# A hybrid pool and RWKV-7 block in float32: output and second feed-forward products by seven block products, tokens on partitions

## The reference

```python
mixed = (g_pool * y_pool + g_rwkv * y_rwkv) @ w_out[l]
x = layer_norm(ALPHA * x + (1 + gt1) * mixed, ln1_g[l], ln1_b[l], LN_EPS)
h = x * (1 + sc2) + sh2
f = jnp.square(jax.nn.relu(h @ w_ff1[l])) @ w_ff2[l]
x = layer_norm(ALPHA * x + (1 + gt2) * f, ln2_g[l], ln2_b[l], LN_EPS)
```

## Time and profile before

| | us |
|---|---|
| median of 3 runs (lowest, highest) | 1109.46 (1108.66, 1114.62) |
| the profiled execution's own time | 1106.47 |
| its span, first to last instruction | 1104.7 |
| PE busy | 999.9 (91%) |
| DVE busy | 517.9 (47%) |
| ACT busy | 413.8 (37%) |
| POOL busy | 401.8 (36%) |
| mean granted clock of PE | 0.957 |

### The profile page before, as it was taken

The page is one execution under the profiler, slowest core; times in us unless marked ns, Lnnn a source line. Parts: engine busy times, 40 slices in busy tenths (PEclk is TensorE's granted clock), DMA queues, the critical chain, the costliest instruction groups (busy, mean ns, idle before and its releaser), DMA issues.

```text
span 1104.7 us, 25425 instructions
## 1 busy us (share of the span) xinstructions
PE 999.9 (91%) x10997; PEld 798.8 (72%) x10997; DVE 517.9 (47%) x620; ACT 413.8 (37%) x500; POOL 401.8 (36%) x236
## 2 busy tenths in 40 slices
PE   1898998898899889997999999889999999999992
PEld 1676777685677678675688888768888888888881
DVE  6636589377748768743231245746112112112217
ACT  0335354356335532524433224375124224214311
POOL 6333412311311131125253443445434434443422
PEclk9799999999999899998899999879999999999996
DMA  9322333223323324321433543304333333333201
GB/s 370 106 77 63 97 117 102 79 79 94 93 79 98 103 60 118 105 76 39 133 100 101 160 114 107 95 1 132 97 94 97 96 96 91 99 95 93 79 1 76
DMA packets 153641, 108.08 MB, mean 98 GB/s; under 512 B 5395, under 2 KB 145601, under 8 KB 153537
## 3 DMA queue, kind: packets, MB, share of 16 engines
q1 hardware_dynamic: 143729, 83.46, 25.9%
q10 hardware_dynamic: 9808, 23.08, 6.9%
HBM read 100.23 MB, written 2.10 MB: 93 GB/s over the span
## 4 chain that ended last, share of the span: by engine, by line
PE 47%; DVE 4%; DMA 1%; ACT 1%; issue 0%; SPq 0%; POOL 0%; DVEq 0%; ACTq 0%; POOLq 0%
PE set L1757 23%; PE bank L1757 20%; PE bank L1859 1%; PE set L1859 1%; DVE G L1319 1%; DMA w_raw<-in_w_rwkv_up_dram 1%; DVE xt L1388 1%; DVE xt L1390 1%; PE set L1821 0%; DVE t L1304 0%; PE set L1838 0%; PE set L1607 0%; PE set L1606 0%; DVE aa L1322 0%; DVE stat L1348 0%
## 5 line engine op out<-in xcount | busy, mean ns | idle before, releaser
L560 POOL TENSOR_TENSOR w_lo<-w_raw,w_hi 128x1024 fp32r<-128x1024 f32 (+2 forms) x87 | 200.4, 2303 | 439.2 <-ACT w_hi L641 399.2
L616 POOL TENSOR_TENSOR w_lo<-w_raw,w_hi 128x1024 fp32r<-128x1024 f32 x48 | 115.8, 2413 | 145.9 <-ACT w_hi L936 145.7
L1460 PE MATMUL bank<-h_hi,w_hi 128*128 128x512 f32 x256 | 109.3, 427 | 2.1 <-POOL w_lo L560 2.0
L641 ACT ACTIVATE w_hi<-w_raw 128x1024 fp32r<-128x1024 f32 (+2 forms) x75 | 75.5, 1006 | 82.9 <-PE set L1757 43.6
L669 ACT ACTIVATE Q<-set 128x1024 f32<-128x1024 f32 x56 | 57.4, 1026 | 130.7 <-PE set L1514 73.8
L936 ACT ACTIVATE w_hi<-w_raw 128x1024 fp32r<-128x1024 f32 x60 | 63.7, 1061 | 110.7 <-PE bank L1757 53.9
L1460 PE MATMUL bank<-h_hi,w_lo 128*128 128x512 f32 x256 | 103.3, 403 | 0.3 <-issue 0.3
L1460 PE MATMUL bank<-h_lo,w_hi 128*128 128x512 f32 x256 | 103.5, 404 | 0.0
L1355 DVE TENSOR_TENSOR f<-t 128x512 f32<-128x512 f32 x32 | 26.4, 825 | 125.9 <-ACT t L945 125.5
L1757 PE MATMUL bank<-h_hi,w_hi 128*128 128x512 f32 x192 | 76.5, 398 | 0.0
L1757 PE MATMUL set<-y_hi,w_hi 128*128 128x512 f32 x192 | 76.1, 396 | 0.0
(11 more groups left out here) (328 smaller groups left out, 2030.3 us busy)
## 6 DMA issues: line engine op xcount, KB each, us to landing
w_raw<-in_w_ff_dram SPq DMA_DIRECT2D x64, 512.0 KB, 3.9
w_raw<-in_w_in_dram SPq DMA_DIRECT2D x46, 512.0 KB, 3.8
y<-in_w_ada_dram ACTq DMA_DIRECT2D x20, 512.0 KB, 4.0
ada<-in_w_ada_dram SPq DMA_DIRECT2D x16, 512.0 KB, 9.6
Q<-in_w_ada_dram ACTq DMA_DIRECT2D x12, 512.0 KB, 4.3
w_raw<-in_w_rwkv_up_dram SPq DMA_DIRECT2D x8, 512.0 KB, 4.3
w_raw<-in_w_out_dram SPq DMA_DIRECT2D x8, 512.0 KB, 3.8
xtok<-in_x_dram SPq DMA_DIRECT2D x4, 512.0 KB, 9.9
```

Of the source, the lines that this page charges most:

```text
L560: link(pool.tensor_tensor(part_of(k, w_lo), part_of(k, w_raw), part_of(k, w_hi).bitcast(F32), ALU.subtract), "lo_ready")
L616: again(pool.tensor_tensor(part_of(k, w_lo), part_of(k, w_raw), part_of(k, w_hi).bitcast(F32), ALU.subtract), "lo_ready")
L641: link(act.activation(part_of(k, w_hi), part_of(k, w_raw), ACT.Copy), "hi_ready")
L1460: mm = pe.matmul(o, w, hx, start=(m == 0), stop=(m == 3 * KT - 1))
```

## The change

**Products.** A 2 x 2 block product is made with seven block products in place of eight. w_out and w_ff2 are cut in units of 512 rows (two units for w_out, eight for w_ff2). A unit's weight is four blocks B11, B12, B21, B22 of 256 x 512 (`load_quarter`, 128 x 1024 in SBUF), and the activations of the unit four blocks by halves of tokens and of rows. Seven sums of each (`FORMS` of weights, seven forms in `a_hi`, `a_lo`) are multiplied. Now the activations are held (128 x 128) and 512 weight columns move, so that tokens are on partitions in the result: 2 token rows x 2 k-tiles x 3 = 12 matmuls for one of the seven, 84 in a unit. A result stays in PSUM and is added to `res` by DVE after each product, to two places in all (`take`, two for each product), so banks are kept open over several products and PE waits for the take between (`FREED_BY`). `FORMS` are split in high and low as the chunks were.

**The order of a feed-forward unit.** PE: four chunks of w_ff1 (24 matmuls each), then the seven products in the order of `PRODUCTS`. There are three slots for `w_hi`/`w_lo`. For each hidden chunk ACT makes ReLU and square and the high parts (`highs`), DVE the sums of token halves and the low parts (`lows`). DVE also multiplies the four weight blocks by the gate row 1 + gt2, which was done on the result before (`scaled`), and makes T1 to T4 (`summed`). Each of these eight is a 128 x 1024 operation on two tiles of SBUF. The first unit stands outside of the loop and also adds the residual, with DVE and POOL.

**Order at the output product.** Its unit 0 comes after n = 5 of the up projections and unit 1 after n = 7. x is loaded straight into `res` and scaled by ACT. Layer norm 1 is made on token rows (`statistics`, `spreads`, `columns`), x hat is turned by PE (32 transposes) and h2 made from that; layer norm 2 likewise, without turning back.

**The tail of the scan.** In the last round the group statistics are made in slot 0, right behind `o_taken`. PE also makes the two gate rows there (`spread_gate`, 8 small matmuls each), and ACT copies them. SP issues the first three weight chunks ahead of the `wmix` tiles; the two broadcast rows are issued later.

```diff
+        FORMS = ("B11", "B21", "T2", "T1", "T3", "B22", "T4")
+        NFORM = len(FORMS)
+        QUARTERS = dict(B11=(3, 0, 0), B12=(4, 0, 1), B21=(5, 1, 0), B22=(6, 1, 1))
+        FORM_RAW = dict(B11=3, B21=5, T2=3, T1=8, T3=4, B22=6, T4=5)
...
+        FIRST_SLOT, SLOT = (1, 2, 0, 2, 0, 1, 2, 0, 1, 2, 0), (1, 2, 1, 2, 0, 1, 2, 0, 1, 2, 0)
+        BEFORE = (8 - PER, 9 - PER, 0, 1, 10 - PER, 2, 3, 4, 5, 6, 7)
+        CHUNK_RAW = (0, 1, 2, 7)
...
+        PRODUCTS = ((0, 4), (2, 0), (5, 4), (4, 6), (1, 4), (6, 6), (3, 4))
+        OPENS = (True, True, False, True, False, False, False)
+        FREED_BY = (6, None, 0, 5, 2, 3, 4)
+        READ_INTO = ((0, 0), (0, 0), (0, 1), (2, 1), (2, 1), (0, 1), (2, 0))
+        SUMS = ("B11", "B12", "B22", "B21", "T1", "T3", "T2", "T4")
+        NSUM = len(SUMS)
+        A_READY = ((1, 3), (2, 4), (5, 7), (5, 7), (6, 8), (6, 8), (6, 8))
...
+            for k in range(K_UP, K_UP + 3):
+                load_chunk(sp, k)
             for g in range(GP):
                 sp.dma_start(wmix[:, g, :], pool_mix[0, g]).then_inc(sem("wmix_in"), 16)
-            sp.dma_start(acc2[:, :], ln2_g.to_broadcast([P, D])).then_inc(sem("ln2_in"), 16)
-            sp.dma_start(ada2[:, :], ln2_b.to_broadcast([P, D])).then_inc(sem("ln2_in"), 16)
-            for k in range(K_UP, K_FF + 2 * KT):
+            for name in ("B11", "B12", "B22", "B21"):
+                load_quarter(sp, 0, name, w_out, 0)
...
+            with pool.Fori(0, NU - 1) as q:
+                again = loop_link(pool, counts, q, {"lo_ready": PER}, "pool_step")
+                for m in range(PER):
+                    pool.wait_ge(sem("hi_ready"), q * PER + (K_FF + PER + m + 1))
+                    raw = w_raw[CHUNK_RAW[m] if m < 4 else FORM_RAW[FORMS[m - 4]]]
+                    again(pool.tensor_tensor(w_lo[SLOT[m]][:, :, :], raw[:, :, :], w_hi[SLOT[m]][:, :, :].bitcast(F32), ALU.subtract), "lo_ready")
...
+            def highs(link, n, base, units=0, per=0):
+
+                i = n % 2
+                if n % 4 < 2:
+                    link(act.activation(a_hi[:, 0, i, :], left[:, i, 0:S // 2], ACT.Copy), "a_hi")
+                    act.wait_ge(sem("a_summed"), units * 4 + (n + 1))
+                    link(act.activation(a_hi[:, 1, i, :], a_sum[:, 0, :], ACT.Copy), "a_hi")
+                else:
+                    link(act.activation(a_hi[:, 2:4, i, :], halves(right[:, :]), ACT.Copy), "a_hi")
+                    act.wait_ge(sem("a_summed"), units * 4 + (n + 1))
+                    link(act.activation(a_hi[:, 4:7, i, :], a_sum[:, 1:4, :], ACT.Copy), "a_hi")
...
+            with act.Fori(0, NU - 1) as q:
+                again = loop_link(act, counts, q, {"hi_ready": PER, "relu": 4, "hidden_raw": 4, "a_hi": 8}, "act_step")
+                for m in range(2):
+                    split_again(again, m, q, 1)
+                for m in range(4):
+                    relu_of(again, m, q, 1)
+                    for k in {0: (2,), 1: (3, 4), 2: (5,), 3: (6,)}[m]:
+                        split_again(again, k, q, 1)
+                    highs(again, 12 + m, 0, q)
+                for m in range(7, PER):
+                    split_again(again, m, q, 1)
...
+                if it == QUADS and s == 0:
+                    link(dve.tensor_reduce(gn[:, 0, :], blocks16(O), AX_X, ALU.add))
+                    link(dve.tensor_scalar(gn[:, 0, :], gn[:, 0, :], 1.0 / N, None, ALU.mult))
+                    link(dve.tensor_tensor(blocks16(O), blocks16(O), gn[:, 0, :].unsqueeze(2).to_broadcast([P, 16, N]), ALU.subtract), "centred")
+                    dve.wait_ge(sem("o_squared"), it)
+                    link(dve.tensor_reduce(gn[:, 1, :], blocks(At), AX_X, ALU.add))
+                    link(dve.tensor_scalar(gn[:, 1, :], gn[:, 1, :], 1.0 / N, GN_EPS, ALU.mult, ALU.add), "o_var")
+                    dve.wait_ge(sem("o_std"), it)
+                    link(dve.reciprocal(gn[:, 3, :], gn[:, 2, :]))
+                    link(dve.tensor_tensor(blocks16(O), blocks16(O), gn[:, 3, :].unsqueeze(2).to_broadcast([P, 16, N]), ALU.mult), "o_normed")
...
+            def lows(link, n, units=0):
+
+                i = n % 2
+                x0, x1 = left[:, i, 0:S // 2], left[:, i, S // 2:S]
+                if n % 4 < 2:
+                    link(dve.tensor_tensor(a_sum[:, 0, :], x0, x1, ALU.subtract), "a_summed")
+                    dve.wait_ge(sem("a_hi"), units * 8 + (2 * n + 1))
+                    link(dve.tensor_tensor(a_lo[:, 0, i, :], x0, a_hi[:, 0, i, :].bitcast(F32), ALU.subtract), "a_low")
+                    dve.wait_ge(sem("a_hi"), units * 8 + (2 * n + 2))
+                    link(dve.tensor_tensor(a_lo[:, 1, i, :], a_sum[:, 0, :], a_hi[:, 1, i, :].bitcast(F32), ALU.subtract), "a_low")
+                else:
+                    link(dve.tensor_tensor(a_sum[:, 1, :], x1, right[:, S // 2:S], ALU.add))
+                    link(dve.tensor_tensor(a_sum[:, 2, :], a_sum[:, 1, :], x0, ALU.subtract))
+                    link(dve.tensor_tensor(a_sum[:, 3, :], right[:, 0:S // 2], a_sum[:, 2, :], ALU.subtract), "a_summed")
+                    dve.wait_ge(sem("a_hi"), units * 8 + (2 * n + 1))
+                    link(dve.tensor_tensor(a_lo[:, 2:4, i, :], halves(right[:, :]), a_hi[:, 2:4, i, :].bitcast(F32), ALU.subtract), "a_low")
+                    dve.wait_ge(sem("a_hi"), units * 8 + (2 * n + 2))
+                    link(dve.tensor_tensor(a_lo[:, 4:7, i, :], a_sum[:, 1:4, :], a_hi[:, 4:7, i, :].bitcast(F32), ALU.subtract), "a_low")
...
+            def scaled(link, name, unit, units=0):
+
+                raw, _, z = QUARTERS[name]
+                dve.wait_ge(sem(f"w_in{raw}"), units * 16 + 16 * (unit + 1))
+                row = (gate1 if unit < 2 else gate2)[:, z * S:(z + 1) * S].unsqueeze(1).to_broadcast([P, 2, S])
+                link(dve.tensor_tensor(two_by(w_raw[raw]), two_by(w_raw[raw]), row, ALU.mult), "summed")
...
+                if name == "T1":
+                    if unit == 3:
+                        dve.wait_ge(sem("lo_ready"), units * PER + (K_UNIT[2] + FORMS.index("T1") + 1))
+                    elif unit:
+                        lo_of("T1", unit - 1)
+                    link(dve.tensor_tensor(made("T1"), b12, made("B11"), ALU.subtract), "summed")
+                elif name == "T3":
+                    link(dve.tensor_tensor(made("T3"), made("B22"), b12, ALU.subtract), "summed")
+                elif name == "T2":
+                    lo_of("B11", unit)
+                    link(dve.tensor_tensor(made("T2"), made("B22"), made("T1"), ALU.subtract), "summed")
+                else:
+                    lo_of("B21", unit)
+                    link(dve.tensor_tensor(made("T4"), made("B21"), made("T2"), ALU.subtract), "summed")
...
+                link(dve.tensor_tensor(res[:, j, half], bank[PRODUCTS[at][1] + row], res[:, j, half], ALU.add), "taken")
...
+            def last_takes(link, unit, stage, units=0):
+
+                for at in range(NFORM - 1):
+                    for row in range(2):
+                        take(link, unit, at, row, units)
+                    if at in (1, 4, 5):
+                        j, z = READ_INTO[at]
+                        statistics(j, z)
+                        statistics(j + 1, z)
+                spreads(0)
+                columns(0, stage)
+                for row in range(2):
+                    take(link, unit, NFORM - 1, row, units)
+                    statistics(2 + row, 0)
+                spreads(1)
+                columns(1, stage)
...
+            def unit_sums(link, units):
+
+                for m in range(4):
+                    dve.wait_ge(sem("hidden_raw"), units * 4 + (4 + m + 1))
+                    lows(link, 12 + m, units)
+                    if m == 0:
+                        scaled(link, "B22", 3, units)
+                        scaled(link, "B21", 3, units)
+                    if m == 1:
+                        summed(link, "T1", 3, units)
+                        summed(link, "T3", 3, units)
+                    if m == 2:
+                        summed(link, "T2", 3, units)
+                    if m == 3:
+                        summed(link, "T4", 3, units)
...
+            with dve.Fori(0, NU - 2) as q:
+                again = loop_link(dve, counts, q, per, "dve_step")
+                unit_sums(again, q)
+                for at in range(NFORM):
+                    for row in range(2):
+                        take(again, 3, at, row, q)
+                    if at == 4:
+                        scaled(again, "B11", 4, q)
+                scaled(again, "B12", 4, q)
...
+                    if it == QUADS:
+                        pe.wait_ge(sem("mods_ready"), 3)
+                        wait_set_free(pe, "gate", it)
+                        spread_gate(1, 16)
+                        spread_gate(0, 40)
...
+            def quarters(unit, k0, slots, free, units=0):
+
+                per_unit = 0 if unit < 3 else 1
```

(92 more changed lines are left out.)

671 lines of the change are left out of this document (348 added, 323 removed).

## The result

The changed kernel takes 1204.52 us (median of 4 runs, 1201.83 to 1209.09) beside 1109.06 us for the kernel before: ratio 1.0856, 95% interval 1.0803 to 1.0910. It is 8.6% slower. The forecast had said slower, 1172 us; its range ended at 1200. The profiled execution took 1209.09 us with a span of 1207.2 us, 102.5 us more than the 1104.7 us of before.

A forecast was written before the change was run, and what follows sets the result against it. PE was taken to bound the kernel before, POOL and DVE's exclusion the changed one: 1106.5 + 64 + 16 - 2 - 7 - 3 - 5.5 = 1169 us, plus 3 for the median, 1172; range 1092 to 1200.

The forecast's parts named there:

- mechanism: Feed-forward units: POOL's splits and DVE's two-SBUF-input operations exclude each other, so PE idles and its clock drops; chance 0.52.
- the start: Before the feed-forward: O comes sooner and the first weight chunk is loaded first; -7 us (0 to -13).
- the price of the residual in the first unit: First feed-forward unit: residual operations on DVE and POOL, put at 7 us.
- First unit: Feed-forward unit outside the loop: a loop unit's excess plus 7 us for the residual; +16 us (0 to +25).
- 7 us on top: First feed-forward unit: allowance for the residual's operations and two chunks at the pace of h2.
- same excess: First feed-forward unit: it lengthens as each loop unit does, by 9.1 us.
- Loop: Seven feed-forward units of 53.4 us, 9.1 more each: +64 us; turns between the last products go: -3 us.
- six stops as counted: Loop unit, before the third product's take: six POOL splits each stop DVE about 2.1 us, 12.6 us in all.
- Tail: After the last product: DVE's chain shortens from 17.6 us to some 13 us; -5.5 us.
- some 13 us with the take: After the last product: DVE's 2.8 us of statistics and six wide operations, one behind POOL, plus the take.
- Output product and norm: Output product and layer norm: 63.8 us with stalls against 66.2 before; -2 us (-12 to +8).
- the 48.8 us: Output product and norm without stalls: matmuls 38.8 us, transposes 3.5, and 6.5 for take, statistics and the norm's other steps.

The follow-up runs named there:

- e4: Changed kernel, with GpSimd's low weight parts of the loop's units made on only 64 of 1024 columns; 1134.77 us (one run).
- e7: Changed kernel, with the first unit's residual scale and shift on 32 of 512 columns, on VectorE and GpSimd; 1190.01 us (one run).
- e8: Changed kernel with eight plain products, no sums, last tail's statistics in late slots, mix weights behind the first weight chunk; 1103.86 us, 0.9940 of the kernel before.

## Why direction and mechanism were right, and the time was not

Direction and mechanism were right, and experiment e4 shows the mechanism. The time was 32 us over the forecast and 4.5 us beyond the range. Between the two profiled executions it is 102.6 us where the sum had 62.5, so 40 us over (the changed kernel's lies 4.6 us above its median, that of before 3 us below). Two steps of the sum failed outright: the start, where the wait that goes was counted and the waits that take its place were not, and the price of the residual in the first unit, 7 us for a measured 16.2. Term by term:

**First unit, +16 forecast, +25 measured.** The mis-sized term is "7 us on top" for the residual: e7 takes off 16.2 us with it, and leaves 8.8 us of excess, as the "same excess" of 9.1 had it. I had counted its operations at free length. In the trace the first four on DVE take 1.66 to 2.71 us each and the gate scalings ahead of them 1.98; of the last four, three are free (0.69) and one takes 2.71. POOL's eight take 1.34 to 2.16 us where 1.29 was counted.

**Start, -7 forecast, +4.6 measured.** This step failed. It took the wait for O to be what would shorten. That wait is gone, and another took its place (6.2 us for POOL's w_lo, behind ScalarE's turn in the statistics). The chunk loads put first pushed the mix's weights late (3.6 us of wait): the prediction priced the load that went forward and not the one that went back. The gate rows cost PE 3.6 us, as forecast (2 to 4). Setting both placements right is worth 6.5 us.

**Loop, +61 forecast, +66.8 measured.** For one unit 53.4 was forecast; the one shown has 54.5, the mean is 54.2. In it 37.8 us to the end of the take measured 38.6: six stops as counted, 11.6 us instead of 12.6, and about 1.8 us more of short waits for ScalarE and gaps. Five products with the clock's share, 13.9 + 1.7, measured 15.85. PE's gap inside the second product was 5.8 us (5 to 6 forecast), DVE was busy 40.07 of 54.45 us (74%, over 65% forecast), POOL 27.6 (26.3). The loop's first six units add 60.1 us (807.03 to 1132.29, against 6 x 44.2) where 54.6 was forecast, and the last one, without the turns, 6.7 where 6.1 was.

**Tail, -5.5 forecast, -0.7 measured.** From the end of the last product DVE's chain is 16.3 us (1186.5 to 1202.8) where the prediction had "some 13 us with the take". It put one of the six wide operations behind POOL; in the trace none of them is, but two small ones of two columns, 1.63 and 1.82 us for 0.17:

```profile
1191.00 1.63 DVE small L1491
...
1193.22 1.82 DVE small L1497
```

**Output product and norm, -2 forecast, +1.8 measured.** By e8 the layout gives 7.4 us, and the seven products cost 9.2 us more in it than eight, by difference. As they have 24 matmuls fewer (5.5 us), their stalls are some 14.7 us, an estimate; 15 was forecast. So the term that was too small is the time without stalls: the 48.8 us and the 5.5 of an eighth product would have been 11.9 us under the 66.2 of before, where e8 gains 7.4.

**Up to the last O, nothing forecast, +5.0 measured.** No edit to the program's order lies there, and it is spread: the other profiles have O between 498.2 and 507.9 us. Before has one profile, at 499.1, so whether the change has a part in it stays open.

The range was too short upwards because it was built from what the loop's unit could be. All six terms missed to the same side, by 40 us in all (9.0 + 11.6 + 5.8 + 4.8 + 3.8 + 5.0), and the loop, on which the prediction had spent its care, by 5.8 of them. That the unit came within 1 us owes something to luck: the stops were 1.0 us shorter than counted and the gaps 1.8 us longer.

## What to carry to other kernels

Fewer products are paid in vector work: count what the saving asks of the engines that feed the matmuls, in exclusive time where two engines share a path, and add what the matmul clock loses when it idles. Cut the change into its layout and its arithmetic before judging it: here eight products in the new layout were level with before, and 0.6% faster once the start's two placements were set right (e8); seven were 7 to 9% slower. When a load or a step is moved forward, price the one that it now stands in front of.

## What the runs showed that I had not expected

Where DVE's operation starts just behind a split, the stop costs about 2.0 us whatever the operation's size: 2.31 us for a sum of 128 columns (0.29 us free) and 3.25 us for the same sum of 1024 (1.23 us free), in the same place. A two-column operation with one tensor input (L1491, 1.63 us for 0.17) was stopped too, which the prediction had only for two inputs in SBUF. The trace of before had a hint of it outside the rows read: a copy of one tile took 2.52 us and ended 0.3 us after a split of POOL (679.44 for 2.39 us; the copy's free length is in no trace):

```profile
679.58 2.52 DVE L1302 COPY t<-t 128x512 f32<-128x512 f32 x1
```

In the last tail's statistics ScalarE loads its table for the square root, and anew behind it (1.28 us at 512.23):

```profile
508.04 1.06 ACT L889 ACTIVATE Q<-O 128x1024 f32<-128x1024 f32 x1 [9.19 <-DVE O L1284]
...
510.70 1.28 ACT L892 ACT_TABLE_LOAD   x1 [1.61 <-DVE gn L1287]
```

A microsecond taken from DVE's chain can be worth more than itself: with T4's sum off the path (1.3 us) the unit fell by 2.2 us on the mean, 1.1 us of it in the 60 matmuls behind the wait. Their time moved with the clock even where the waits were the same (14.1 to 15.9 us), so this part is not shown to follow from the shorter wait.
